# The output projection of a two-layer hybrid trunk as three float32r products

## The reference

```python
for l in range(DEPTH):                                    # two layers
    h = rmsnorm(x, pre_norm[l])
    proj = jnp.einsum('bld,de->ble', h, w_in[l])          # D_MODEL = 1024
    # gated DeltaNet, SSD and retention over chunks, each with an RMSNorm and a SiLU gate:
    ...
    mixed = jnp.concatenate([o_a, o_b, o_c], axis=-1)     # (1, 1024, 2048): o_a 512, o_b 1024, o_c 512 wide
    out = jnp.einsum('ble,ed->bld', mixed, w_out[l])      # the output projection, 2048 x 1024
    x = x + rmsnorm(out, post_norm[l])
```

## Time and profile before

| | |
|---|---|
| median of 3 runs | 2578.44 us (2575.63 to 2580.75) |
| time of the profiled execution | 2574.64 us |
| its span, first to last instruction | 2572.8 us |
| TensorE busy | 2375.9 us, 92% of the span |
| VectorE / ScalarE / GpSimd busy | 1328.1 / 836.7 / 912.8 us |
| mean granted TensorE clock | 0.971 |
| data moved by DMA | 175.72 MB, mean 68 GB/s |

### The profile page before, as it was taken

The page is one execution under the profiler, slowest core; times in us unless marked ns, Lnnn a source line. Parts: engine busy times, 40 slices in busy tenths (PEclk is TensorE's granted clock), DMA queues, the critical chain, the costliest instruction groups (busy, mean ns, idle before and its releaser), DMA issues.

```text
span 2572.8 us, 37761 instructions
## 1 busy us (share of the span) xinstructions
PE 2375.9 (92%) x15352; PEld 2136.4 (83%) x15352; DVE 1328.1 (52%) x2268; ACT 836.7 (33%) x1565; POOL 912.8 (35%) x757
## 2 busy tenths in 40 slices
PE   5899999999898999999889899999989899899995
PEld 4788979898687887989878788899977789788994
DVE  3655455634455555553545555654354664566333
ACT  3534323213343432222333343222224343332220
POOL 3544412323244451232324554222324454322220
PEclk9999989999999998999989999999999999899997
DMA  3111102222122110222223111022222211111212
GB/s 122 57 65 50 66 25 66 82 67 85 64 98 75 63 53 33 66 75 79 80 80 106 59 50 66 25 66 79 73 72 89 107 66 50 50 50 50 75 58 90
DMA packets 33276, 175.72 MB, mean 68 GB/s; under 512 B 3728, under 2 KB 4272, under 8 KB 19664
## 3 DMA queue, kind: packets, MB, share of 16 engines
q1 hardware_dynamic: 32832, 171.85, 19.5%
q0 software_dynamic: 272, 1.45, 0.2%
HBM read 164.90 MB, written 8.39 MB: 67 GB/s over the span
## 4 chain that ended last, share of the span: by engine, by line
PE 77%; DVE 8%; issue 7%; ACT 5%; POOL 2%; DMA 1%; SPq 0%; DVEq 0%; ACTq 0%; POOLq 0%
PE ps L628 73%; PE ps L631 4%; POOL w_low L1555 1%; DVE slot L985 1%; ACT slot L1362 1%; ACT wk L1384 1%; ACT raw L1333 1%; DVE wk L1056 0%; DMA bc<-x_mid 0%; DMA row<-in_rows 0%; ACT w_hi L1307 0%; DVE bc L985 0%; DVE acc L1258 0%; DVE wk L1060 0%; DVE acc L1260 0%
## 5 line engine op out<-in xcount | busy, mean ns | idle before, releaser
L1555 POOL TENSOR_TENSOR w_low<-w_loaded,w_hi 128x512 fp32r<-128x512 f32 x416 | 547.8, 1333 | 675.0 <-ACT w_hi L1307 674.3
L628 PE MATMUL ps<-w_hi,hT_hi 128*128 128x256 f32 x1792 | 540.6, 302 | 0.0
L628 PE MATMUL ps<-w_low,hT_hi 128*128 128x256 f32 x1792 | 506.5, 283 | 0.0
L628 PE MATMUL ps<-w_hi,hT_lo 128*128 128x256 f32 x1792 | 501.2, 280 | 0.0
L628 PE MATMUL ps<-wo_loaded,mixT 128*128 128x256 f32 x2048 | 470.7, 385 | 23.1 <-DVE mixT L1158 23.1
L628 PEld LDWEIGHTS ps<-wk 128*128 128x128 f32 x2976 | 392.4, 199 | 103.4 <-ACT wk L1384 52.3
L628 PE MATMUL ps<-wk 128*128 128x128 f32 (+2 forms) x2976 | 424.5, 289 | 56.4 <-ACT wk L1384 41.1
L628 PEld LDWEIGHTS ps<-wo_loaded,mixT 128*128 128x128 f32 x2048 | 391.1, 194 | 87.1 <-issue 37.7
L628 PEld LDWEIGHTS ps<-w_low,hT_hi 128*128 128x128 f32 x1792 | 341.8, 191 | 3.6 <-issue 1.0
L628 PEld LDWEIGHTS ps<-w_hi,hT_hi 128*128 128x128 f32 x1792 | 338.1, 189 | 3.6 <-issue 1.0
L628 PEld LDWEIGHTS ps<-w_hi,hT_lo 128*128 128x128 f32 x1792 | 340.9, 190 | 0.0
(11 more groups left out here) (181 smaller groups left out, 2708.8 us busy)
## 6 DMA issues: line engine op xcount, KB each, us to landing
w_loaded<-in_w_in SPq DMA_DIRECT2D x104, 1024.0 KB, 4.9
wo_loaded<-in_w_out SPq DMA_DIRECT2D x64, 512.0 KB, 3.5
wk<-in_x SPq DMA_DIRECT2D x8, 512.0 KB, 3.8
...
```

What stands on the lines that cost most here:

```text
L628: return nc.tensor.matmul(o, a, b, start=start, stop=stop)
L1555: tt(w_lo[at], wr[at], w_hi[at], ALU.subtract)\
```

## The change

The output projection is computed like the input projection. Each unit's weights are split after their transfer: a new step `split_out` has ScalarE copy two halves of 512 columns into `wo_hi`, and GpSimd subtract them and put the low part where the weights were loaded (`wo_parts`). `mixT` becomes `mixT_hi` and `mixT_lo`, for which VectorE does one product over the bank and four products with a subtraction over its quarters. Each matmul of an out step becomes three. `make_plan` puts the first unit's `split_out` right behind `mix_turn`, and each further one behind the last out step of the unit before; in the last burst a little earlier. TensorE waits for a unit's low halves at its first and third k block. To make room, GpSimd's DMA scratch is made smaller, and the loads of the constants move from GpSimd's queue to ScalarE's. The rest of the list of steps is the same, in the same order.

```diff
@@ -172,6 +172,7 @@
         rest[0] = 4 if s[0] == "ssd_l" and s[3] == 0 else pause.get(s[0], 1)
         if s[0] == "mix_turn":
             outs.extend(("out", s[1], s[2], u, tp) for u in range(UNITS) for tp in range(NT // 2))
+            split_next(outs)
             if s[2] == GROUPS - 1:
 
                 q = s[1]
@@ -185,10 +186,20 @@
             if rest[0] > 1:
                 flush_outs(1)
 
-    def flush_outs(n):
+    def split_next(out):
+
+        if out and out[0][0] == "out" and ("split_out", *out[0][1:4]) not in done:
+            emit(("split_out", *out[0][1:4]))
+
+    def flush_outs(n, last=False):
         while outs and n:
-            emit(outs.pop(0))
+            s = outs.pop(0)
+            emit(s)
             n -= 1
+            if s[0] == "out" and s[4] == NT // 2 - 1:
+                split_next(outs)
+            elif last:
+                split_next([o for o in outs if o[0] == "out"][1:])
 
     for p in range(PARTS):
         if p >= 2:
@@ -252,7 +263,7 @@
     while at[0] < len(mix):
         assert mix_one(True)
         flush_outs(1)
-    flush_outs(99)
+    flush_outs(99, True)
     return plan
@@ -379,6 +390,7 @@
 
         hT_hi, hT_lo = sb("hT_hi", KD, HALF, dtype=F32R), sb("hT_lo", KD, HALF, dtype=F32R)
         w_hi = sb("w_hi", W_RING, KD * PC, dtype=F32R)
+        wo_hi = sb("wo_hi", 2, 4 * PC, dtype=F32R)
         raw = sb("raw", 2, 3 + HALF)
         halo = sb("halo", 24, 3)
         slot = sb("slot", SLOTS, 4 * HALF)
@@ -386,7 +398,7 @@
 
         xfin, post = (bc[:, 2 * i:2 * i + 2, :].rearrange("p a b -> p (a b)") for i in range(2))
         gate = sb("gate", 2, NT, 512)
-        mixT = sb("mixT", 4, HALF)
+        mixT_hi, mixT_lo = sb("mixT_hi", 4, HALF, dtype=F32R), sb("mixT_lo", 4, HALF, dtype=F32R)
         acc = sb("acc", NT, D)
         st_g = sb("st_g", GH, P)
         st_s = sb("st_s", SG, 512)
...
@@ -693,15 +706,20 @@
                         close(i, tag)
                 elif k == "out":
                     G, u, tp = s[2:]
-                    w = wo[:, unit_no[s[:4]] % 2, :].rearrange("p (k n) -> p k n", k=4)
+                    r = unit_no[s[:4]] % 2
+                    lo, hi = (a[:, r, :].rearrange("p (k n) -> p k n", k=4) for a in (wo_parts, wo_hi))
                     b = opened(s)
-                    if tp == 0:
-                        loaded_unit(pe, s[:4])
                     for v in range(2):
                         t = 2 * tp + v
                         wait_emptied(pe, ("mix_turn", p, G, t))
                         for kk in range(4):
-                            i = mm(b[:, v * PC:(v + 1) * PC], mixT[:, kk, t * P:(t + 1) * P], w[:, kk, :], kk == 0, kk == 3)
+                            if tp == 0 and v == 0 and kk % 2 == 0:
+                                pe.wait_ge(S["wo_lo_ready"], 2 * out_no[s[:4]] + kk // 2 + 1)
+                            m_hi, m_lo = (m[:, kk, t * P:(t + 1) * P] for m in (mixT_hi, mixT_lo))
+                            o = b[:, v * PC:(v + 1) * PC]
+                            mm(o, m_hi, hi[:, kk, :], kk == 0, False)
+                            mm(o, m_hi, lo[:, kk, :], False, False)
+                            i = mm(o, m_lo, hi[:, kk, :], False, kk == 3)
                     close(i, s)
                 elif k == "gdn_decay":
                     h = s[2]
@@ -1155,8 +1173,12 @@
                     for t in range(NT):
                         tag = (*s, t)
                         wait_filled(dve, tag)
-                        empty(tt(mixT[:, :, t * P:(t + 1) * P], bank4(tag), over_cols(par[:, l, Q_MIX + 4 * s[2]:Q_MIX + 4 * s[2] + 4]),
-                                 ALU.mult), tag)
+                        at, q = slice(t * P, (t + 1) * P), Q_MIX + 4 * s[2]
+                        chain(tt(mixT_hi[:, :, at], bank4(tag), over_cols(par[:, l, q:q + 4]), ALU.mult))
+                        for j in range(4):
+                            ins = stt(mixT_lo[:, j, at], bank4(tag)[:, j, :], par[:, l, q + j:q + j + 1], mixT_hi[:, j, at],
+                                      ALU.mult, ALU.subtract)
+                        empty(ins, tag)
                 elif k == "out":
                     G, u, tp = s[2:]
                     wait_filled(dve, s)
@@ -1277,6 +1299,10 @@
                     act.wait_ge(*junk_read.pop())
                 junk_read.append(read_by)
 
+            act.dma_start(con[:], cons).then_inc(loaded, 16)
+            for l in range(DEPTH):
+                act.dma_start(par[:, l, :], pars[l]).then_inc(loaded, 16)
+                act.dma_start(row[:, l, :], rows[l].partition_broadcast(P)).then_inc(loaded, 16)
             act.wait_ge(loaded, 16 * (1 + 2 * DEPTH))
             A(nega[:], row[:, :, R_A:R_A + NDEC], ACT.Exp).then_inc(S["nega_ready"], 1)
             for s in plan:
@@ -1306,6 +1332,15 @@
                             wait_filled(act, ("proj", *divmod(n - W_RING, len(PIECES)), 1))
                     A(w_hi[:, n % W_RING, j * 512:(j + 1) * 512], wr[:, n % W_RING, j * 512:(j + 1) * 512], ACT.Copy)\
                         .then_inc(S["w_hi_ready"], 1)
+                elif k == "split_out":
+                    u = ("out", *s[1:])
+                    r = unit_no[u] % 2
+                    loaded_unit(act, u)
+                    if unit_no[u] >= 2:
+                        wait_filled(act, unit_use(units[unit_no[u] - 2]))
+                    for j in range(2):
+                        at = slice(j * 2 * PC, (j + 1) * 2 * PC)
+                        A(wo_hi[:, r, at], wo[:, r, at], ACT.Copy).then_inc(S["wo_hi_ready"], 1)
                 elif k == "split_small":
                     loaded_unit(act, ("small", p))
                     w, _, hi = wsm_parts(p)
@@ -1467,10 +1502,6 @@
                 m = con[:, C_LEV + lv * P:C_LEV + (lv + 1) * P]
                 tt((bT0, bT1)[lv % 2], aT, over_rows(m), ALU.mult).then_inc(S["gdn_masks"], 1)
 
-            pool.dma_start(con[:], cons).then_inc(loaded, 16)
-            for l in range(DEPTH):
-                pool.dma_start(par[:, l, :], pars[l]).then_inc(loaded, 16)
-                pool.dma_start(row[:, l, :], rows[l].partition_broadcast(P)).then_inc(loaded, 16)
             pool.wait_ge(loaded, 16 * (1 + 2 * DEPTH))
             for s in plan:
                 k, p = s[0], s[1]
@@ -1554,6 +1585,13 @@
                     at = (slice(None), n % W_RING, slice(j * 512, (j + 1) * 512))
                     tt(w_lo[at], wr[at], w_hi[at], ALU.subtract)\
                         .then_inc(S["w_lo_ready"], 1)
+                elif k == "split_out":
+                    u = ("out", *s[1:])
+                    r = unit_no[u] % 2
+                    for j in range(2):
+                        pool.wait_ge(S["wo_hi_ready"], 2 * out_no[u] + j + 1)
+                        at = slice(j * 2 * PC, (j + 1) * 2 * PC)
+                        tt(wo_parts[:, r, at], wo[:, r, at], wo_hi[:, r, at], ALU.subtract).then_inc(S["wo_lo_ready"], 1)
                 elif k == "split_small":
                     pool.wait_ge(S["wsm_hi_ready"], p + 1)
                     w, lo, hi = wsm_parts(p)
@@ -1596,7 +1634,7 @@
     rows = np.concatenate([f["gdn_A_log"], f["ssd_A_log"], f["gdn_dt_bias"], f["ssd_dt_bias"], f["ssd_D"]], axis=1)
     cons, rope = constants()
 
-    nc = bacc.Bacc("TRN2", target_bir_lowering=False, num_devices=1)
+    nc = bacc.Bacc("TRN2", target_bir_lowering=False, num_devices=1, dynamic_dma_scratch_size=1024)
     arrays = {"x": f["x"].reshape(SEQ, D), "w_in": wl, "w_small": ws, "w_out": wol, "cons": cons, "rope": rope, "pars": pars, "rows": rows,
               "post": f["post_norm"]}
     arrays = {f"in_{k}": np.ascontiguousarray(v) for k, v in arrays.items()}
```

3 lines of the change are left out of this document (2 added, 1 removed).

## The result

The changed kernel takes 2615.2 us (median of 4 runs, 2612.9 to 2619.1), the kernel before on the same chip 2577.5 (2575.6 to 2580.8): a ratio of 1.0147, with a 95% interval from 1.0129 to 1.0164. I had predicted 2562 us and a small gain. It is 38 us slower, outside my range and on the other side. Of the gain of 78 us that I had counted, all went and 38 more, so 116 us were given back where I had counted 62 (an estimate: the 78 are my own sum).

The account below looks back on a forecast made before the run. TensorE, busy 92% of the span, was taken as the bound. 78 us saved on out steps less 62 us given back left 16 us gained, so 2562 us predicted; the range leaving out 2 in 10 was 2544 to 2586.

Parts of the forecast that it names:

- The gain of 78 us: TensorE's 128 out steps: each falls from 3.45 us to 2.82 to 2.88, saving 73 to 81 us, taken as 78.
- First step of group 1: TensorE waits there for the halves of the low weights, behind ScalarE's gate eviction: loss 1.9 us, four times, 7.6.
- Of group 2: First step of group 2: halves come late behind an eviction that needs a table load; loss 3.1 us, four times, 12.4.
- my clock term: Idle gaps lower TensorE's granted clock: 2 us three times at the 4.9 us gap, 3 us at group 2's; 9 us.
- Of group 3: First step of group 3, parts 0 to 2: 1.5 us for GpSimd's splits, 1.1 for the first mixT tile; 7.8 us.
- Late splits of group 3: Fourth unit's split stands behind the last gdn_decay; loss 5.5 us in three parts, 16.5, the largest single item.
- The third unit's wait: Group 3's third unit waits behind the decay before it in the same way: 1.4 us, 4.2 in all.
- Group 1's fourth unit: A late split there, found by the same walk: loss 0.6 us in each part, 2.4 us in all.
- Group 0's first step: Row tiles of mixT come later behind their transposes: estimated loss 0.7 us, four times, 2.8 us.
- The step that failed: Ssd stretch, fourth chunk's y product: TensorE arriving 0.6 us earlier buys little, 2 us given back.
- The second rival, slower by the clock: Each of 14 new gaps pays 2.55 us through the lower clock: 2589 us; chance 0.16.
- The rule that I had weighed: GpSimd contends with VectorE's two-SBUF-input instructions, so 165 us of subtractions could hold VectorE; rival: 18 us, 2578 us, chance 0.15.

Follow-up runs that it names:

- `products_alone`: Changed kernel keeping only the float32r products: mixT written once, weights' high parts made for the first two units alone, no subtraction; 2512.7 us.
- `no_subtraction`: Changed kernel without GpSimd's subtraction for the output projection; the second product reads the high parts and waits for ScalarE's copy alone; 2547.1 us.
- `subtraction_unread`: As `no_subtraction`, but GpSimd makes the subtraction at its old place and no product reads it or waits for it; 2590.8 us.
- `before_plus_splits`: Kernel before, float32 products kept, plus ScalarE's copies and GpSimd's subtractions at the changed kernel's places, unread by the products; 2609.9 us.

## Why the prediction was wrong, step by step

*The gain of 78 us* was right. In the last burst of `products_alone` the 192 matmuls follow each other at 0.118 us, so 2.84 us a step, and TensorE's shorter work gives 66 us when hardly anything else is changed.

*First step of group 1*: forecast 1.9 in each part. The profile after has a wait of 0.90 us and one of 0.21 for the second half, and a step that ends about 1.5 late. Right. *Of group 2*: forecast 3.1; the wait is 2.46 us and the step then runs at low clock, about 4.0 in all. The mechanism is right; with its share of my clock term (3 us in four parts) I had 3.85. *Of group 3*: 10.8 us of wait instead of 7.7, forecast 2.6 and measured 3.1 in the wait. Right, and in both of its parts: 9.0 us in `no_subtraction` and 10.8 in `subtraction_unread`, so 1.3 without GpSimd's splits (forecast 1.1) and 1.8 by them (forecast 1.5).

*Late splits of group 3*: the wait of the fourth unit was expected to be 4.9 us, and 4.9 is the longest wait for wo_parts in the trace, with 40.1 in total where I had set 20 to 60. Lateness as a whole costs 24 us by experiment, and going early removes the wait. The third unit's wait is 0.8 us instead of my 1.4. My walk along the queues gave this well.

*Group 1's fourth unit*: forecast 0.6 in each part. This term is mis-sized: the waits are 1.48 and 0.64 us, and with the low clock behind them it is about 4. The walk did not see that GpSimd's skip term stands in front of the subtraction and is itself held, 1.50 instead of 1.04 us (at 1113.27 in part 1; the subtractions follow it, and TensorE waits for them at 1116.13).

*Group 0's first step*: I priced only mixT there, 2.8 us in all. The split stands right behind `mix_turn` in the plan; GpSimd has nothing to do in `mix_turn`, comes to it early, and holds VectorE's operations on the way to the transposes: 2.1 us in each part, 8 in all, which were in no term.

*The step that failed* has two halves. The first is *"In the ssd stretch ... it buys little: 2 us"*, which asked what TensorE's 0.6 us would be worth at one chunk and did not ask whether VectorE and GpSimd could follow. The second is a term that the sum did not have: apart from 1.5 us at group 3's first step, GpSimd's subtractions cost VectorE nothing in it. From the transposes of group 0 to those of group 1, the stretch with four of the chunks, part 1 took 68.7 us before and takes 72.1 now, though its eight output steps are 4.9 us shorter (the first fence is before, the second after):

```profile
987.85 2.56 PE L631 MATMUL ps<-con,gate 128*128 128x128 f32 x16 [2.27 <-DVE gate L1136]
...
1056.56 1.69 PE L631 MATMUL ps<-con,gate 128*128 128x128 f32 x14
```
```profile
999.01 1.33 PE L644 MATMUL ps<-con,gate 128*128 128x128 f32 x5 [4.34 <-DVE gate L1154]
...
1071.14 1.91 PE L644 MATMUL ps<-con,gate 128*128 128x128 f32 x16
```

The same distances, from the first transposes of one group to those of the next, summed over the four parts, are these (us, one profiled execution of each kernel; in the first two rows the parts of a kernel differ by up to 4 us). The second column is the first less the 19.5 us by which a group's steps are shorter.

| transposes of | before | less 19.5 | `products_alone` | `no_subtraction` | `subtraction_unread` | changed |
|---|---|---|---|---|---|---|
| group 0 to 1 | 271.4 | 251.9 | 265.9 | 279.7 | 282.3 | 284.3 |
| group 1 to 2 | 288.2 | 268.7 | 268.7 | 274.0 | 297.6 | 290.9 |
| group 2 to 3 | 581.8 | 562.3 | 563.7 | 568.6 | 575.0 | 582.0 |
| group 3 to the next part's 0, or the end | 1074.9 | 1055.4 | 1056.0 | 1066.6 | 1082.8 | 1100.0 |

Group 0's stretch gives back 32 us (284.3 against 251.9), where I had 2 for the ssd stretch and 2.8 for the first step. But 14 of them are there with the products alone: where my term had 2 us, nearly all that does not land of the 78 is lost, since TensorE, which never idled in this stretch before, now waits there for the masked gram. Another 14 come with the two parts of mixT and ScalarE's copies; I have not separated these. The subtraction's presence adds no more than 3 here. It costs in group 1's stretch (24 us) and in group 3's (16, with the gates ahead of the next part's group 0), and in group 2's (6). With the products waiting for the subtraction, 7 of group 1's come back and 7 and 17 are lost in the last two rows; why group 1's come back I have not followed. Where it costs also depends on what else runs: in `before_plus_splits`, with float32 products, group 0's stretch is 23 us longer than before and group 1's is unchanged.

My other terms, the clock's 9 us among them, come to 60 us; mixT, copies and lateness measure 59 (34.4 and 24.4, below). So the sum failed by what it left out, 44 us, and by the ssd term, 2 us instead of some 13.

*The clock*: I had 9 us. Time at the low level rose by 86 us (from 149 to 235, above), each of which costs up to half a microsecond of matmuls. No experiment changes the clock and leaves the gaps as they are, so I leave its own size open; it is at most 43 us. The second rival, slower by the clock, had the sign and not the account.

*The rule that I had weighed* was the right one, and I gave it the wrong weight. I made it a rival with a chance of 0.15 and priced it by averages: a third of a third of 165 us. The measured price is 44 of 172 us, a quarter. The averages missed that VectorE's own operations are not evenly spread: the splits stand just behind the output steps, and in group 1's stretch that is where the ssd chain has little room.

The sum by experiment, each from one kernel to the next: 2578 - 78 = 2500 would be the full gain. 12.7 do not land (2512.7, `products_alone`). Two parts of mixT, ScalarE's copies and the waits for them give 34.4 (2547.1), of which 12 to 13 are mixT and the wait for wo_hi is 13.1; the rest I have not separated. The subtraction's presence gives 43.7 (2590.8), nearly all of it by what it holds on VectorE, as the waits say, and its lateness 24.4 (2615.2). That is 115 of the 116 us. These are differences of medians from several chips, on which the kernel before differs by up to 4 us; by the ratios the four are 13, 32, 46 and 25.
